# Two attention stages of a two-layer diffusion trunk, written as flat sequences of units with their outputs kept in SBUF

## The reference, cut to what matters

```
# layer 0, 8 heads of two 64-wide halves m
s = einsum('bqhmd,bkhmd->bhmqk', qb, kk) * scale
p = softmax(s, axis=-1)
a = p[:, :, 0] - lam * p[:, :, 1]
o = einsum('bhqk,bkhe->bqhe', a, vv)                 # vv 128 wide
y = (_rmsnorm(o, sub_g) * (1 - lam_init)).reshape(...) @ wo
# image queries see 1024 + 256 keys, context queries the 256 context keys
# layer 1, 16 query heads on 4 key heads; only image queries
s_loc = where(|q - k| <= 128, q.k * scale, -1e30)    # at most 3 blocks of 128 keys
s_ctx = q.kc * scale                                 # 2 blocks
p = softmax([s_loc, s_ctx, sink])[..., :-1]
y = (p @ [v, vc]) @ wo
```

## Time and profile before

| | us |
|---|---|
| median of 3 runs | 3397.03 (3390.61 to 3397.22) |
| the profiled execution, its own time | 3395.04 |
| its span, first to last instruction | 3393.2 |
| front of layer 0 ends, attention begins | 538.46 |
| first output product of layer 0 complete (DVE takes it) | 1085.05 |
| attention of layer 1 begins | 2210.67 |
| first output product of layer 1 complete | 2576.97 |

### The profile page before, as it was taken

One profiled execution on the slowest core, in us unless ns is written; L12 is line 12 of the kernel. 1 busy time (PEld: TensorE's weight loads), 2 busy tenths in 40 slices (PEclk: granted clock), 3 DMA queues, 4 the chain that ended last, 5 costly groups with the idle time before them and its releaser, 6 DMA issues. The chain is left out here.

```text
span 3393.2 us, 38136 instructions
## 1 busy us (share of the span) xinstructions
PE 2917.1 (86%) x13041; PEld 1628.0 (48%) x13041; DVE 1286.9 (38%) x2390; ACT 814.1 (24%) x1819; POOL 548.0 (16%) x767
## 2 busy tenths in 40 slices
PE   7999995999996966999999859968888859999982
PEld 3444333888883533444444324457774424443431
DVE  4444112777774243111111165367772341110114
ACT  2211002766673000000000043145551000000000
POOL 2455100111112110000000035400001100000000
PEclk8999997999998977999999979989999869999996
DMA  6333668322225328999999383254443289999985
GB/s 240 97 99 130 223 232 195 65 50 43 49 49 183 132 89 348 416 387 413 384 413 391 150 297 118 62 114 91 90 113 134 95 362 422 426 427 426 427 378 207
DMA packets 256876, 760.81 MB, mean 224 GB/s; under 512 B 31216, under 2 KB 176544, under 8 KB 220656
## 3 DMA queue, kind: packets, MB, share of 16 engines
q1 hardware_dynamic: 152160, 642.51, 50.6%
q10 hardware_dynamic: 89296, 78.90, 7.4%
q0 software_dynamic: 15296, 37.78, 2.8%
HBM read 678.57 MB, written 98.37 MB: 229 GB/s over the span
## 5 line engine op out<-in xcount | busy, mean ns | idle before, releaser
L1823 PE MATMUL psum<-moe_ring,moe_xT 128*64 128x512 f32 (+1 forms) x2240 | 705.4, 600 | 15.6 <-DMA moe_ring<-in_e_w 13.3
L391 PE MATMUL psum<-qkv_w,act_hT 128*128 128x512 f32 x1376 | 611.8, 598 | 0.1
L1823 PEld LDWEIGHTS psum<-moe_ring,moe_xT 128*64 128x64 f32 (+1 forms) x2240 | 276.4, 161 | 408.8 <-issue 406.8
L391 PEld LDWEIGHTS psum<-qkv_w,act_hT 128*128 128x128 f32 x1376 | 257.0, 192 | 306.9 <-issue 306.9
L1844 PE MATMUL psum<-moe_ring,moe_hT 128*64 128x512 f32 (+1 forms) x1120 | 352.8, 594 | 1.6 <-DVE moe_hT L1924 1.6
L1107 ACT ACTIVATE att_prob<-psum,att_nmax 128x1280 f32<-128x1280 f32 (+3 forms) x288 | 283.8, 986 | 114.3 <-DVE att_nmax L1221 66.9
L1920 DVE TENSOR_TENSOR moe_hh<-psum,moe_sg 128x512 f32<-128x512 f32 x50 | 34.6, 692 | 665.9 <-PE psum L1823 665.9
L1381 PE MATMUL psum<-post_wo,post_oT 128*128 128x512 f32 x576 | 258.1, 603 | 22.3 <-DMA post_wo<-in_a_wo 14.1
L954 PE MATMUL psum<-att_kT,att_q 128*128 128x512 f32 (+1 forms) x832 | 211.5, 391 | 47.7 <-ACTq L1202 26.3
L1221 DVE TENSOR_REDUCE att_nmax<-psum 128x1 f32<-128x1280 f32 (+1 forms) x160 | 204.3, 1278 | 113.6 <-PE psum L954 111.1
L1844 PEld LDWEIGHTS psum<-moe_ring,moe_hT 128*64 128x64 f32 (+1 forms) x1120 | 133.1, 160 | 184.6 <-issue 180.4
(11 more groups left out here) (248 smaller groups left out, 3101.2 us busy)
## 6 DMA issues: line engine op xcount, KB each, us to landing
moe_ring<-in_e_w SPq DMA_DIRECT2D x216, 2048.0 KB, 16.6
ada_w<-in_ada_w SPq DMA_DIRECT2D x48, 1024.0 KB, 6.4
att_q<-qk_d SPq DMA_DIRECT2D x144, 256.0 KB, 4.8
qk_d<-qkv_stg ACTq DMA_DIRECT2D x112, 256.0 KB, 2.5
qkv_w<-in_a_wqkv SPq DMA_DIRECT2D x6, 2048.0 KB, 8.9
prep_y<-y_d SPq DMA_DIRECT2D x10, 1024.0 KB, 6.5
o_d<-att_oTs ACTq DMA_DIRECT2D x18, 512.0 KB, 2.8
post_oT<-o_d SPq DMA_DIRECT2D x18, 512.0 KB, 4.6
```

Source lines behind the costliest of these rows:

```text
L391: ins = nc.tensor.matmul(psum[:, u.par, :], hT[:, k, u.t * P:(u.t + 1) * P], qw[:, u.C % 2, k], start=(k == 0), stop=(k == KD - 1))
L1823: ins = nc.tensor.matmul(psum[part, bank, :], xT[:, 4 * half + k, part], ring[:, w13[x, half] % RING, k, bank * DE:(bank + 1) * DE], start ...
```

## The change

Both attention stages become flat sequences, without loops and without a restart between tiles.

- Layer 0 goes head by head: `UNITS0` lists ten tiles for head 0, then ten for head 1, so that eight full units are followed by two short ones, eight times. Keys and queries of one head are loaded together (`load_head`, 3.9 MB in eight DMAs of 64 partitions, packets of 5120 B), in two buffers. Head 0 is loaded by SP within the front, behind piece 24 of `ada_w`; head 1 at the stage's start; head h when the scores of head h-2 are done.
- The middle piece of the transposes is copied by DVE instead of ACT. Two one-element steps move from DVE to POOL (the product `epsum`, and its addition to the sum of squares), and PE waits for the first (`s_mixp`).
- Outputs go to `oT`, which stays in SBUF for the post stage; `o_d` and its stores and loads go. `wo` is loaded during the attention, in layer 0 behind the scores of head 6 and in layer 1 behind the first queries.
- Layer 1 keeps all keys (`kall`, 2.6 MB, loaded once between the two halves of the first queries) and V (`vstg`) in SBUF; `v_d` goes. The wait for the third piece stands before the last block's products.
- The loops of the post stage are written out.

```
 # sp_front, layer 0
             for n in range(11, 48):
                 load_ada(sp, n)
+                if n == 24:
+                    sp.wait_ge(s_qev, 42)
+                    for par in range(2):
+                        sp.wait_ge(s_qst[par], 16 + 32 * 20)
+                    load_head(sp, 0)
 # layer 1
-        for t in range(TA):
-            sp.wait_ge(s_vev, t + 1)
-            sp.dma_start(v_d[t * P:(t + 1) * P, :], vstg[:, t, :]).then_inc(s_vst, 16)
...
+    UNITS0 = [(h, t) for h in range(KD) for t in range(TA)]
+    UNITS1 = [(t, j) for t in range(TX) for j in range(KD)]
+    def load_head(sp, h):
+        buf = (h + 1) % 2
         for part in range(2):
             for m in range(2):
+                sp.dma_start(kT[buf][64 * part:64 * part + 64, m].bitcast(F32), qk_d[KD + h, part, 64 * m:64 * m + 64, :]).then_inc(s_kq[buf], 16)
+        for rows in range(2):
+            for m in range(2):
+                sp.dma_start(aq0[buf][64 * rows:64 * rows + 64, m].bitcast(F32), qk_d[h, :, 64 * m:64 * m + 64, :].rearrange("x d n -> d x n")).then_inc(s_kq[buf], 16)
+    def sp_att0(sp):
+        load_head(sp, 1)
+        for h in range(2, KD):
+            sp.wait_ge(s_score, 2 * TA * (h - 1))
+            load_head(sp, h)
+        sp.wait_ge(s_score, 2 * TA * (KD - 1))
+        load_wo(sp, 0)
+    def sp_att1(sp):
+        load_q(sp, 0, 0)
+        ...  # kall: four DMAs
+        load_q(sp, 0, 1)
+        load_wo(sp, 1)
+        ...
 # pe_att0, unit n
+            pe.wait_ge(s_mix, n + 1)
+            ...
+            if full:
+                blocks(n, 4, 8, 7).then_inc(s_turn[1], 1)
+                pe.wait_ge(s_mixp, n + 1)
+            scores(n + 2, 0)
+            pe.wait_ge(s_took[0], n + 1)
+            ins = blocks(n, 8, 10, 6) if full else None
+            if n >= 2:
+                ins = turn_output(n - 2, 2)
+            ...
+            if full:
+                pe.wait_ge(s_took[1], full_before(n) + 1)
+            for b in range(nb):
+                if b == 8:
+                    pe.wait_ge(s_took[2], n + 1)
+                ...  # product with V
+            scores(n + 2, 1)
 # dve_att0
+        for n, (h, t) in enumerate(UNITS0):
+            peak(n + 1, 0)
+            weigh(n)
+            if n:
+                copy_output(n - 1)
+            peak(n + 1, 1)
+            if t < TX:
+                dve.wait_ge(s_turn[1], full_before(n) + 1)
+                nc.vector.tensor_copy(aT0[:, n % 2, 4:8, :], psum[:, 7, :].rearrange("p (b n) -> p b n", n=P)).then_inc(s_took[1], 1)
 # pool_att0, per unit
+            pool.wait_ge(s_coef, n + 1)
+            ins = nc.gpsimd.tensor_scalar(epsum[:, q], den[:, q, 0:1], den[:, q, 0:1], EPS, ALU.mult, ALU.mult)
+            ins.then_inc(s_mixp, 1)
+            ...  # then unit n-1: ssq + epsum, power, scaling
 # pe_att1
+            pe.wait_ge(s_took[1], FULL0 + n + 1)
             for b in range(nb):
+                if b == 4:
+                    pe.wait_ge(s_took[2], N0 + 1 + n + 1)
 # post
-            sp.dma_start(oT[:, par].rearrange("p k n -> p (k n)"), o_d[ds(t, 1)].rearrange("o p n -> p (o n)")).then_inc(s_pin[par], 16)
-            if isinstance(t, int) and t == 0 and l == 0:
-                load_wo(sp, l)
-            pe.wait_ge(s_pin[par], pin_count(T, par))
```

More of the change, by code:

```diff
@@ L69, in build @@
     qk_d = dram("qk_d", [16, 2, P, NTOK])
-    v_d = dram("v_d", [NTOK, 256])
-    o_d = dram("o_d", [TA, P, D])
     xs_d = dram("xs_d", [NTOK, D])
@@ L176, in tile_steps @@
     def tile_steps(eng, tiles, step, chain=None, links=0):
-        step(0, 0)
-        step(1, 1)
-        def body(i):
-            for par in range(2):
-                step(2 * i + 2 + par, par)
-        trips(eng, TX // 2 - 1, body, chain, 2 * links)
-        for t in range(TX, tiles):
+        for t in range(tiles):
             step(t, t % 2)
@@ new lines, in sp_att1 @@
+    def sp_att1(sp):
+        load_q(sp, 0, 0)
+        for part in range(2):
+            for m in range(2):
+                sp.dma_start(kall[64 * part:64 * part + 64, m:4:2].bitcast(F32), qk_d[8:10, part, 64 * m:64 * m + 64, :].rearrange("h d n -> d h n")).then_inc(s_kq[0], 16)
+        load_q(sp, 0, 1)
+        load_wo(sp, 1)
+        for t in range(1, TX):
+            for half in range(2):
+                sp.wait_ge(s_score, 2 * N0 + 2 * (8 * (t - 1) + 4 * half + 4))
+                load_q(sp, t, half)
@@ new lines, in pe_att0, with scores, blocks @@
+    def pe_att0(pe):
+        def scores(n, m):
+            if n >= N0:
+                return
+            h, t = UNITS0[n]
+            buf = (h + 1) % 2
+            if t == 0 and m == 0:
+                pe.wait_ge(s_kq[buf], 128 * (h // 2 + 1))
+            if n:
+                pe.wait_ge(s_exp, 2 * (n - 1) + m + 1)
+            for b, (lo, hi) in enumerate(((0, 512), (512, 1024), (1024, 1280)) if t < TX else ((SEQ, NTOK),)):
+                for x in range(2):
+                    ins = nc.tensor.matmul(psum[:, 3 * m + b, 0:hi - lo], aq0[buf][:, m, x, t * P:(t + 1) * P], kT[buf][:, m, lo:hi], start=x == 0, stop=x == 1)
+            ins.then_inc(s_score, 1)
+        def blocks(n, lo, hi, bank):
@@ L1351, in pin_count @@
     def pin_count(T, par):
-        return 16 * (T - par + 2)
+        return 8 * (T - par + 2)
     def pe_post(pe, l):
```

712 lines of the change are left out of this document (276 added, 436 removed).

## The result

| | before | after | difference | forecast |
|---|---|---|---|---|
| median of all runs, us | 3397.03 | 3274.16 (3273.79 to 3276.18) | 122.9 less | 122 less |
| the profiled execution, its span | 3393.20 | 3272.20 | 121.0 less | 122.0 less |
| front of layer 0, to the stage's first load | 538.46 | 550.75 | 12.3 more | 10.5 more |
| attention 0, to the first output product taken | 546.59 | 461.91 | 84.7 less | 85.6 less |
| from there to attention 1 | 1125.62 | 1124.62 | 1.0 less | 0 |

The ratio is 0.9644, 95% interval 0.9627 to 0.9661. Each row after the second is read between two marks: SP's first load of a stage, and DVE taking the first output product. The five differences add up to the 121.0 of the spans. The kernel before, timed again beside the experiments, had medians of 3392.80 to 3397.03, so a few us between medians mean little and small differences are read from the stages.

A forecast was written before the change was run, and what follows sets the result against it. PE was taken to bound layer 0's attention inside tile pairs, two waits layer 1's wide units. Gains 85.6 and 46.9 minus a front loss of 10.5 made 122.0, so 3275 us (own range 3258 to 3292; 8 in 10: 3246 to 3318).

The forecast's parts named there:

- Front, 10.5 more: Layer 0's front: PE stalls 9.3 us for piece 25 behind head 0's loads, plus 1.2 at low clock.
- Full units 5.90, PE-bound: Layer 0's attention: full units stay 5.90 us apart (ends 5.85 and 6.2), PE's work, with DVE at 5.76.
- It just fits: Layer 0's full units: DVE's middle copy is done at 2.44 to 2.5 us, PE reaches the products at 2.5.
- rival 2: DVE becomes the bound of layer 0's full units: 6.3 us per unit, 26 us more, 3301; chance 0.13.
- The step on POOL costs nothing: Layer 0's attention: PE needs POOL's `epsum` 2.5 us after it begins; 0.6 early even after waiting out the weighing.
- Four drains, about 45: Layer 0's attention: removing the four drains at tile pairs' ends gives about 45 us of the 85.6 gained.
- Store and wait for `wo` in layer 0, about 20: End of layer 0's attention: dropping the output store and the wait for `wo` gives 20 us of the gain.
- Mixing short and full units, minus 19: Layer 0's attention: short units placed among full ones take 19 us off the gain.
- 1: Layer 1's third copy was not the limit of wide units; another 0.6 us wait shows: 3301 us, chance 0.13.
- 3: Layer 0's front: the head's loads don't stall it, giving 3264 us; chance 0.09.
- 4: Flat code makes engines stand still at instruction blocks; at 4 us each the time is 3415 us; chance 0.03.
- 5: Units don't overlap across tiles, so only starts and ends gain: 3346 us; chance 0.07, shared with another case.

The follow-up runs named there:

- Experiment 3: Kernel after the change, with head 0's eight loads issued by ScalarE on its own queue instead of SP's: 3273.70 us (0.9637).
- experiment 6: Kernel after the change, with the middle copy of the transposed blocks back on ScalarE instead of VectorE: 3270.64 us (0.9639).
- experiment 5: Kernel after the change, with `epsum` computed on VectorE instead of POOL, in four buffers instead of two: 3274.69 us (0.9649).
- experiment 11: Kernel after the change, with three breaks in layer 0's sequence, at units 20, 40 and 60: 3287.15 us (0.9679).
- Experiment 4: Kernel after the change, with both layers' output weights loaded only when the output stage begins: 3292.76 us (0.9696).
- experiment 1: Kernel after the change, with layer 1's wait for the third piece back in front of all products with V: 3302.21 us (0.9723).
- experiment 12: Kernel after the change, with layer 1's keys loaded by four DMAs writing 128 partitions each instead of 64: 3312.97 us (0.9768).

## Why the prediction was right, and where it was off

- *Front, 10.5 more.* Measured 12.3, and 13.6 between the means of the kernels with the loads in a row and spread. The mechanism was right (wait for piece 25, then low clock); the wait was 11.5 and not 9.3, since the piece landed at 444.2 (forecast 443) and PE wanted it at 432.7 (433.7), and the low clock cost 1.9 and not 1.2. That piece 25 came behind the eight loads agrees with the queue order that the forecast counted on. Experiment 3 bounds it: the order is a part of the loss; on the other queue 10.5 of the 13.6 stayed.
- *PE begins at once in layer 0, fill 10.5.* 0.03 and 11.1.
- *Full units 5.90, PE-bound.* Mis-sized: 5.84, and PE's own work is 5.76 (experiment 6). The old 5.90, whose groups stand without a gap, was taken for PE's work, but 0.14 of it was not. That a short wait behind a group doesn't show there because the ends of matmuls are modelled is argued; no run of the old order tells it apart. "It just fits" was off by 0.08: the middle copy does pace PE, rival 2's mechanism, at 0.08 a unit and not at the 0.4 priced there.
- *Heads 54.6.* 54.5: full units shorter, units 7 to 10 14.2 and not 13.7. Two errors that cancel.
- *The step on POOL costs nothing.* Right (experiment 5 moves it back: 0.2 in the stage), though it lasts as long as the weighing (below), the case for which the forecast had 0.6 to spare in full units. At each head's end PE does wait 0.93 for it; in experiment 5 PE waits there 0.71 for the weighing and then 0.26 for an exponent, which is the same.
- *First product 15.0 behind the barrier.* 16.3 in layer 0, where the clock is low at first, 14.1 in layer 1.
- *Late start, about 37.* 38: PE's first scores 21.1 sooner, 3.6 less from them to the first result, and 13.2 in one distance, where PE of the kernel before waited for queries:

```profile
599.62 2.50 PE L954 MATMUL psum<-att_kT,att_q 128*128 128x512 f32 x6 [11.86 <-DMA att_q<-qk_d]
```

- *Four drains, about 45.* 46 by the distances of L1257 (13.3, 14.3, 13.0 and, into the short units, 5.7); by the estimate at experiment 11 about half of each of the first three is the pipeline's emptying.
- *Store and wait for `wo` in layer 0, about 20.* Too large: from the last result to the first output product the kernel before took 33.5 us and the kernel after 20.1, so 13. *Mixing short and full units, minus 19.* Too large as well: minus 13.5 against the old distances. These two errors of some 6 us cancel. In layer 1 the stage's end gave 9.9 (forecast 8). Experiment 4 puts 17.7 of these 23 on the weights.
- *Attention 1: loads 19.7, fill 13.4.* 19.9 and 13.3. *Wide units 4.45*: 4.37, right at the low end of 4.35, since PE and not DVE closes the loop. The distances from the first result to the last sum to 266.5 (forecast 270.6); with the last copy and the first product that gives the 5.3 us by which the stage beat its forecast.
- *Nothing elsewhere.* 3.6 more, most of it scatter of the last stretch. The three stretches together gave 124.6 where 122.0 were forecast, so the total's agreement within 1 us is in part luck, as is that of layer 0's attention (84.7 for 85.6), whose terms were off by up to 7.
- *Rivals.* 1 fell (experiment 1). 2 is true in kind, at a fifth of its price. 3 fell: the stall is there. 4 fell: 1.9 us of waiting on issue in the weight loads of 80 units; the sequences cost nothing that shows. 5 fell: units overlap across tiles and heads.

## What to carry to other kernels

When a wait for several pieces of work closes a loop, put it in front of the first use of the last piece; here that one line was worth 28 of 123 us. A transfer moved ahead among other loads is best cut up and spread between them: 3.9 MB in a row cost 13.6 us, the same bytes in eight places next to nothing (how small the parts must be wasn't tried). And units of unlike size cost at each change from one kind to the other, here 3.1 us a pair, so sort them by kind, even if some operands must be loaded twice.

## What the runs showed of the hardware

POOL's step on one number per row takes as long as the DVE step that runs beside it. POOL's timeline, in the kernel after,

```profile
610.23 0.56 POOL L868 TENSOR_SCALAR att_epsum<-att_den 128x1 f32<-128x1 f32 x1 [1.37 <-DVE att_coef L1000]
...
614.75 1.62 POOL L868 TENSOR_SCALAR att_epsum<-att_den 128x1 f32<-128x1 f32 x1 [1.57 <-DVE att_coef L1000]
616.96 0.19 POOL L859 TENSOR_TENSOR att_ssq<-att_ssq,att_epsum 128x1 f32<-128x1 f32 x1 [0.59 <-ACT att_osq L955]
...
990.40 0.27 POOL L868 TENSOR_SCALAR att_epsum<-att_den 128x1 f32<-128x1 f32 x1
```

and DVE's weighing, which has two inputs in SBUF:

```profile
610.17 0.48 DVE L1003 SCALAR_TENSOR_TENSOR att_prob<-att_prob,att_coef 128x256 f32<-128x256 f32 x1
...
614.69 1.55 DVE L1003 SCALAR_TENSOR_TENSOR att_prob<-att_prob,att_coef 128x1280 f32<-128x1280 f32 x1
...
989.86 0.48 DVE L1003 SCALAR_TENSOR_TENSOR att_prob<-att_prob,att_coef 128x256 f32<-128x256 f32 x1
```

1.62 beside 1.55, 0.56 beside 0.48, and 0.19 for a step as small (the addition) that runs beside DVE's maximum, which reads PSUM. The last line of each view is the control: in one unit of 80 POOL began at 990.40, just after the weighing had ended at 990.34, and the same step took 0.27. DVE's own step is not longer than the 1.55 of the earlier trace rows. The Trainium skill says in "GPSIMD Engine Reference", section "1. Specifications", that POOL's interfaces to SBUF are shared with VectorE and contend with steps of two SBUF inputs. The trace agrees, and adds that here, where DVE begins 0.06 sooner, POOL alone pays.

The other is experiment 12: DMAs whose source falls into two blocks ran at 53 GB/s, a quarter of the 213 of the earlier trace rows that such loads reach with 64 rows outermost.
